# The inverse of the delta rule: both 64-row halves of a product in one PSUM bank, and one instruction to empty it

## The reference

```python
k_beta = kc * bc[..., None]
kk = jnp.einsum('nbhik,nbhjk->nbhij', k_beta, kc) * seg
a_mat = jnp.eye(L, dtype=F32) + jnp.where(strict, kk, 0.0)
rhs = jnp.concatenate([v_beta, k_beta * jnp.exp(b)[..., None]], axis=-1)
sol = lax.linalg.triangular_solve(a_mat, rhs, left_side=True, lower=True)
u, w = sol[..., :V], sol[..., V:]
...
def step(S, xs):
    v_new = u_c - jnp.einsum('bhik,bhkv->bhiv', w_c, S)
    o = jnp.einsum('bhik,bhkv->bhiv', q_d, S) + jnp.einsum('bhij,bhjv->bhiv', a_c, v_new)
    S = S * jnp.exp(bl)[..., None] + jnp.einsum('bhjk,bhjv->bhkv', k_o, v_new)
    return S, o
```

## Time and profile before

| what | us |
|---|---|
| three runs, median (lowest to highest) | 2605.27 (2598.81 to 2605.86) |
| span of the profiled execution | 2602.8 |
| PE busy in it | 2444.8 (94%) |
| DVE, ACT, POOL busy | 1348.7, 916.7, 785.7 |
| `phase_mix_c`, first key transpose to the end | 1750.05 to 2602.8 |
| one steady tile of it, from Y(0,0) to the next Y(0,0) | 2058.16 to 2105.30, so 47.14 |

### The profile page before, as it was taken

One profiled execution on the slowest core, in us unless ns is written; L12 is line 12 of the kernel. 1 busy time (PEld: TensorE's weight loads), 2 busy tenths in 40 slices (PEclk: granted clock), 3 DMA queues, 4 the chain that ended last, 5 costly groups with the idle time before them and its releaser, 6 DMA issues. The chain is left out here.

```text
span 2602.8 us, 53223 instructions
## 1 busy us (share of the span) xinstructions
PE 2444.8 (94%) x20756; PEld 1476.9 (57%) x20756; DVE 1348.7 (52%) x2949; ACT 916.7 (35%) x2636; POOL 785.7 (30%) x847
## 2 busy tenths in 40 slices
PE   6989999997999977999999999987999999999998
PEld 2434444444565533444444444456787887878876
DVE  3422222122678844992634626436566675666666
ACT  3633232322111114442322322235455554544541
POOL 2540000021111103550000000007456465565554
PEclk8999999998999997999999999998999999999998
DMA  8541212134544553551121121126222231221313
GB/s 296 156 142 45 89 49 77 42 121 138 210 153 147 172 178 111 164 153 66 65 74 49 61 88 49 57 67 192 73 91 83 67 107 59 83 91 59 95 35 94
DMA packets 254517, 270.02 MB, mean 104 GB/s; under 512 B 30263, under 2 KB 188023, under 8 KB 254314
## 3 DMA queue, kind: packets, MB, share of 16 engines
q1 hardware_dynamic: 186762, 219.27, 25.8%
q10 hardware_dynamic: 67552, 47.84, 6.7%
HBM read 179.70 MB, written 87.36 MB: 103 GB/s over the span
## 5 line engine op out<-in xcount | busy, mean ns | idle before, releaser
L625 PE MATMUL inc_b<-raw_next,inc_w_hi 128*128 128x512 bf16 (+1 forms) x768 | 229.9, 381 | 1.6 <-POOL inc_w_lo L574 1.6
L625 PE MATMUL inc_b<-keep,inc_w_hi 128*128 128x512 bf16 (+1 forms) x768 | 228.4, 379 | 0.0
L625 PE MATMUL inab_b<-inab_wt,keep 128*128 128x512 f16 x768 | 168.4, 381 | 10.6 <-POOL inab_wt L574 10.6
L625 PE MATMUL inab_b<-inab_wt,raw_next 128*128 128x512 f16 x768 | 166.4, 379 | 0.0
L1171 PE MATMUL mixab_y<-keep,mixab_oT_hi 128*128 128x512 f16 x512 | 153.4, 381 | 7.4 <-DVE mixab_f_y L1251 5.7
L2173 DVE SCALAR_TENSOR_TENSOR inc_acc<-inc_ub,inc_taps,inc_acc 128x512 f32<-128x512 f32 x192 | 152.1, 792 | 6.8
L625 PE MATMUL inc_b<-raw_next,inc_w_lo 128*128 128x512 bf16 x384 | 146.3, 381 | 0.0
L625 PE MATMUL inc_b<-keep,inc_w_lo 128*128 128x512 bf16 x384 | 145.6, 379 | 0.0
L2071 ACT ACTIVATE inc_ub<-inc_b 128x512 f32<-128x512 f32 x96 | 56.9, 593 | 251.1 <-PE inc_b L625 251.1
L2169 DVE COPY inc_ub<-inc_halo 128x3 f32<-128x3 f32 x96 | 26.1, 272 | 228.1 <-ACT inc_ub L2071 228.1
L625 PEld LDWEIGHTS inab_b<-inab_wt,keep 128*128 128x128 bf16 (+1 forms) x768 | 75.4, 98 | 101.4 <-issue 13.2
(11 more groups left out here) (590 smaller groups left out, 6085.4 us busy)
## 6 DMA issues: line engine op xcount, KB each, us to landing
tmp_qkv<-stage_next SPq DMA_DIRECT2D x98, 256.0 KB, 2.0
stage_next<-in_w_in_c ACTq DMA_DIRECT2D x30, 512.0 KB, 4.5
inab_stage<-in_w_in_ab ACTq DMA_DIRECT2D x24, 512.0 KB, 4.0
raw_next<-tmp_qkv SPq DMA_DIRECT2D x8, 1536.0 KB, 6.9
mixc_qkv<-tmp_qkv SPq DMA_DIRECT2D x8, 1536.0 KB
inab_wt<-in_w_ada SPq DMA_DIRECT2D x10, 1024.0 KB, 14.7
keep<-in_x_prompt SPq DMA_DIRECT2D x16, 512.0 KB, 4.1
tmp_v<-inab_vz SPq DMA_DIRECT2D x32, 256.0 KB, 4.1
```

The costliest lines, as they stand in the source:

```text
L625: last = nc.tensor.matmul(dst, lhs(a, k), rhs(b, k), start=(k == 0 and i == 0), stop=(k == KT - 1 and i == len(PASSES) - 1))
```

## The change

Both halves of a product go to one bank, at their own partitions: Y to A0 (g = 0) or C0 (g = 1), T and N to B0 (g = 0) or C1 (g = 1). One DVE instruction over 128 partitions writes `Y`, one ACT instruction copies `T`, and one copies `N`; DVE's copies of `T` and `N` at levels 0 to 3 go. So that an instruction over 128 partitions can write both halves of `N`, the inverse stays in the compact `N0` through the levels, and the last level's result alone is copied to `N` (low half by ACT, high half by DVE, now the full 64 columns). `first_inverse` goes, and `tn_products` of level 0 waits for `N0` itself. `y_product` no longer waits for copies of `N`. The keys of g = 1 are transposed first, into B1, which the levels leave free. All matmuls remain.

```diff
-    LY = [[half_view(x)[:, 0:4] for x in pair] for pair in ((A0, A1), (C0, C1))]
-    LT = [[half_view(x)[:, 0:4] for x in pair] for pair in ((B0, B1), (C0, C1))]
-    LN = [[half_view(x)[:, 4:8] for x in pair] for pair in ((B0, B1), (C0, C1))]
+    LY = [half_view(x)[:, 0:4] for x in (A0, C0)]
+    LT = [half_view(x)[:, 0:4] for x in (B0, C1)]
+    LN = [half_view(x)[:, 4:8] for x in (B0, C1)]
...
-        def first_inverse(t, halves):
...
         def evacuate(t, k, g, halves, widths):
...
-            if not final or w == LEVELS[-1]:
-                act.activation(blocks(T[HALF[0], gs(g), :], w, 0), blocks(LT[g][0][HALF[0]], w, 0), ACT.Copy).then_inc(t_lo, 1)
-            if not final and g == 0 and 1 in halves:
-                act.wait_ge(t_hi, nth(t, g, NL - 1, k))
-            for e in halves if g == 0 else LOW:
-                last = act.activation(blocks(N[HALF[e], gs(g), HALF[e]], w, 1), blocks(LN[g][e][HALF[e]], w, 1), ACT.Copy)
-            last.then_inc(n_ready, 1)
+            if not last_width or w == LEVELS[-1]:
+                rows = HALF[0] if last_width or halves == LOW else slice(0, P)
+                act.activation(blocks(T[rows, gs(g), :], w, 0), blocks(LT[g][rows], w, 0), ACT.Copy).then_inc(t_copied, 1)
+            if last_width:
+                act.activation(N[HALF[0], gs(g), HALF[0]], LN[g][HALF[0]], ACT.Copy).then_inc(n_low, 1)
+            else:
+                act.activation(blocks(N0[rows, gs(g), :], w, 1), blocks(LN[g][rows], w, 1), ACT.Copy).then_inc(n_copied, 1)
...
-        for g in GRP:
+        for g in KEY_GRP:
             key_squares(0, 0, P, g)
             key_copy(0, 0, P, g)
         last_decay(0, 0, 0, P)
         for g in GRP:
             decays(0, 0, P, g)
-        first_inverse(0, BOTH)
         query_squares(0, P)
...
-            for e in halves:
-                rows = HALF[e]
-                last = dve.tensor_tensor(blocks(Y[w][rows, gs(g), :], w, 0), blocks(LY[g][e][rows], w, 0),
-                                         bc(eye[rows], [HB, 4, HB // (2 * w), w]), ALU.add)
-            last.then_inc(y_ready, 1)
...
+            dve.tensor_tensor(blocks(Y[w][rows, gs(g), :], w, 0), blocks(LY[g][rows], w, 0),
+                              bc(eye, [HB if halves == LOW else P, 4, HB // (2 * w), w]), ALU.add).then_inc(y_ready, 1)
...
+            if k == len(widths) - 1 and 1 in halves:
                 dve.wait_ge(tn_mm, nth(t, g, NL, k))
-                dve.tensor_copy(blocks(T[HALF[1], gs(g), :], w, 0), blocks(LT[g][1][HALF[1]], w, 0)).then_inc(t_hi, 1)
-            if 1 in halves and g == 1:
-                dve.wait_ge(tn_mm, nth(t, g, NL, k))
-                dve.tensor_copy(blocks(N[HALF[1], gs(g), HALF[1]], w, 1), blocks(LN[g][1][HALF[1]], w, 1)).then_inc(n1_hi, 1)
+                dve.tensor_copy(N[HALF[1], gs(g), HALF[1]], LN[g][HALF[1]]).then_inc(n_high, 1)
...
-        dve.wait_ge(n0_copied, nth(nt, 1))
+        dve.wait_ge(tn_mm, nth(nt, 1, NL, 1))
...
-                if 1 in halves:
-                    pe.wait_ge(t_hi, nth(t, g, NL - 1, k - 1))
-                if g == 1:
-                    evacuated(t, k - 1, g, halves)
-                wait_apart(pe, t_lo, nth(t, g, NL, k - 1), fin.tick)
+                wait_apart(pe, t_copied, nth(t, g, NL, k - 1), fin.tick)
...
-                pe.wait_ge(n0_copied, nth(t, g))
+                pe.wait_ge(n0_ready, nth(t, g))
             else:
-                evacuated(t, k - 1, g, halves)
+                pe.wait_ge(n_copied, nth(t, g, NL - 1, k - 1))
...
-                        mm(LT[g][e][rows, i, :], N[rows, h, rows], Y[w][rows, h, :], start=True, stop=True)
-                    last = mm(LN[g][e][rows, i, :], Y[w][rows, h, :], N[rows, h, rows], start=True, stop=True)
+                        mm(LT[g][rows, i, :], N0[rows, h, :], Y[w][rows, h, :], start=True, stop=True)
+                    last = mm(LN[g][rows, i, :], Y[w][rows, h, :], N0[rows, h, :], start=True, stop=True)
...
                 if k == 2:
-                    turn_k(t + 1, nxt, half, n2, 0)
+                    turn_k(t + 1, nxt, half, n2, 1)
...
-            turn_k(t + 1, nxt, half, n2, 1)
+            turn_k(t + 1, nxt, half, n2, 0)
```

More of the change, by code:

```diff
@@ L2402, in phase_mix_c @@
         "gram", "qk_done", "ebl_ready", "lsub", "lseg_ready", "seg_ready", "segw_ready", "bt_ready", "attn_ready"))
[L2403 to L2406, removed]
+    n0_half, n0_ready, t0_ready, btm_ready, y_init = (s(n) for n in (
+        "n0_half", "n0_ready", "t0_ready", "btm_ready", "y_init"))
+    y_mm, y_ready, tn_mm, t_copied, n_copied, n_low, n_high = (s(n) for n in (
+        "y_mm", "y_ready", "tn_mm", "t_copied", "n_copied", "n_low", "n_high"))
     y64_mm, y64_ready, n64_mm, n64_ready = s("y64_mm"), s("y64_ready"), s("n64_mm"), s("n64_ready")
@@ L2895, in y_part, with n_part @@
             w = widths[k]
-            eye = blocks(tv["eye_h"].unsqueeze(1), w, 0)
+            rows = HALF[0] if halves == LOW else slice(0, P)
+            eye = blocks(tv["eye_h"][rows].unsqueeze(1), w, 0)
             dve.wait_ge(y_mm, nth(t, g, NL, k))
-            for e in halves:
-                rows = HALF[e]
-                last = dve.tensor_tensor(blocks(Y[w][rows, gs(g), :], w, 0), blocks(LY[g][e][rows], w, 0),
-                                         bc(eye[rows], [HB, 4, HB // (2 * w), w]), ALU.add)
-            last.then_inc(y_ready, 1)
-        def t_part(t, k, g, halves, widths):
-            w = widths[k]
-            if 1 in halves and k < len(widths) - 1:
+            dve.tensor_tensor(blocks(Y[w][rows, gs(g), :], w, 0), blocks(LY[g][rows], w, 0),
+                              bc(eye, [HB if halves == LOW else P, 4, HB // (2 * w), w]), ALU.add).then_inc(y_ready, 1)
+        def n_part(t, k, g, halves, widths):
+            if k == len(widths) - 1 and 1 in halves:
                 dve.wait_ge(tn_mm, nth(t, g, NL, k))
-                dve.tensor_copy(blocks(T[HALF[1], gs(g), :], w, 0), blocks(LT[g][1][HALF[1]], w, 0)).then_inc(t_hi, 1)
-            if 1 in halves and g == 1:
-                dve.wait_ge(tn_mm, nth(t, g, NL, k))
-                dve.tensor_copy(blocks(N[HALF[1], gs(g), HALF[1]], w, 1), blocks(LN[g][1][HALF[1]], w, 1)).then_inc(n1_hi, 1)
+                dve.tensor_copy(N[HALF[1], gs(g), HALF[1]], LN[g][HALF[1]]).then_inc(n_high, 1)
         def levels(t, halves, widths, beside=lambda k: None):
@@ L3097, in turn_k @@
             pe.wait_ge(tile_in[par], 32 * (half + 1) if not isinstance(t, int) or t else 16)
-            if t:
-                pe.wait_ge(t_lo, nth(t - 1, 0, NL, NL - 1))
-                pe.wait_ge(n_ready, nth(t - 1, 0, NL, NL - 1))
+            if t and g == 1:
+                pe.wait_ge(attn_ready, nth(t - 1, 1))
+            elif t:
+                pe.wait_ge(t_copied, nth(t - 1, 0, NL, NL - 1))
+                inverse_ready(t - 1, 0)
             for i, h in heads(g):
@@ L3140, in turn_o, with inverse_ready @@
                 last.then_inc(o_turned, 1)
-        def evacuated(t, k, g, halves):
-            pe.wait_ge(n_ready, nth(t, g, NL, k))
-            if g == 1 and 1 in halves:
-                pe.wait_ge(n1_hi, NL * t + k + 1)
+        def inverse_ready(t, g):
+            pe.wait_ge(n_low, nth(t, g))
+            pe.wait_ge(n_high, nth(t, g))
         def y_product(t, k, g, halves, widths):
@@ L3162, in y_product @@
                     rows = HALF[e]
-                    last = mm(LY[g][e][rows, i, :], BTm[w][rows, h, :], T[rows, h, :], start=True, stop=True)
+                    last = mm(LY[g][rows, i, :], BTm[w][rows, h, :], T[rows, h, :], start=True, stop=True)
             last.then_inc(y_mm, 1)
@@ L3177, in tn_products @@
                     rows = HALF[e]
[L3178 to L3180 removed]
+                    if not last_width or (w == LEVELS[-1] and e == 0):
+                        mm(LT[g][rows, i, :], N0[rows, h, :], Y[w][rows, h, :], start=True, stop=True)
+                    last = mm(LN[g][rows, i, :], Y[w][rows, h, :], N0[rows, h, :], start=True, stop=True)
             last.then_inc(tn_mm, 1)
@@ L3210, in across_n @@
         def across_n(t):
-            evacuated(t, NL - 1, 1, BOTH)
+            for g in GRP:
+                inverse_ready(t, g)
             wait_apart(pe, y64_ready, t + 1, fin.tick)
```

36 lines of the change are left out of this document (15 added, 21 removed).

## The result

The kernel after takes 2574.53 us (median of 4 runs, 2569.45 to 2583.57) beside 2605.57 for the kernel before on the same chip (4 runs). The ratio is 0.9888, with a 95% interval from 0.9864 to 0.9911. 2571 was predicted, with 2560 to 2588 as the range. The sum went by the span, and there the agreement looks better still: 2568.6 against 2567.6. In part that is luck: the profiled execution was the fastest of the four, and its agreement hides errors that cancel, as the stretches of the phase show. The kernel after was profiled twice; the second execution is that of the run `c4_after_again`, the same program on another chip.

What follows compares the result with a forecast made beforehand. PE bounds the kernel: fully busy for 26.70 us of a steady tile, with waits in the 20.44 us of levels. 16 tiles at 1.91 (30.6) plus 3.6 ahead of tile 0 save 34.2 us: 2571 us, range 2560 to 2588.

Steps and rivals of the forecast that it cites:

- rival 1: Levels: halves writing one bank take turns, 12 us a tile more, 192 in all, near 2797 us; chance 0.09.
- Y by one instruction: Level rounds: one DVE instruction takes 0.29 us, so TN(k,1) starts 1.27 after Y(k,1) rather than 1.57.
- The N wait: Ahead of Y(k,1) in the levels: without waiting for DVE's N copy, it starts 0.95 us behind TN(k,0), 0.18 less.
- Beyond the two waits above this is worth nothing in a steady tile: Steady tile: removed DVE and ACT work gains nothing besides the Y and N waits; it lies beside PE's work.
- The text's own floor: One level round without waiting: two TN groups of 0.95 and two Y groups of 0.58, 3.06 us against 3.65.
- The end of the levels: From Y(4,1) to TN(4,1), key transpose between: 1.27 us in place of 1.56, 0.29 saved per tile.
- Ahead of tile 0: Before Y(0,0) of tile 0: without first_inverse the query squares start earlier, 3.6 us saved (bounds 0 and 5.71).
- The sample tile has low halves only and gains nothing: Sample tile, after the 16 prompt tiles: the change is worth nothing there.
- The part on moved work: DVE and ACT copies dropped or widened, keys of g = 1 first: worth nothing in a steady tile beyond the two waits.
- Rival 2: Level rounds: only one of the two waits goes, 11.5 or 10 us less gain, 2583 or 2581 us; chance 0.13.
- rival 3: Steady tile: no change that can be told, the gaps reappear in PE's 26.70 us of projection work; chance 0.03.
- Rival 4: Stalls of issue, 3.16 us in tile 1, shift the time a few us either way; widens the range, no chance given.

Runs made afterwards that it cites:

- c2_all_but_bank: Kernel after with everything undone (two Y instructions, copies shared out, old key order, ScalarE's first copies) except the one bank and N's compact target: 2617.46 us, ratio 1.0053.
- c1_copies_split: Kernel after with the levels' T and N copies shared out over ACT and DVE as before, with PE's waits for them; one bank kept: 2595.47 us, ratio 0.9963.
- b2_n_wait: Kernel after with PE's wait for ACT's copy of N(k-1,1) put back ahead of Y(k,1): 2575.85 us, ratio 0.9884.
- a2_before_wait: Kernel before with one added wait: DVE's identity-pair copy waits for the sample tile's last TN group: 2614.66 us, ratio 1.0032 to the kernel before.
- b1_y_two: Kernel after with DVE's Y again by two instructions, one per 64-partition half, out of one bank: 2591.0 us, ratio 0.9936.
- b4_key_order: Kernel after with the next tile's keys transposed in the old order, heads 0 to 3 first: 2581.62 us, ratio 0.9911.
- b3_first_copies: Kernel after with ACT's first_inverse copies of N0 restored at their old places in every tile: 2577.05 us, ratio 0.9881.
- a3_pool_behind: Kernel after with POOL's residual add of the last tile but one held back until DVE's first four decayed-state products are done: 2570.89 us, ratio 0.9863.
- a4_eye_own: Kernel after with the identity pair in SBUF space of its own, so its copy keeps its place without the wait for PE: 2566.26 us, ratio 0.9839.

## Why the prediction was right, and where it was wrong

**Two halves in one bank (rival 1): right.** The groups keep their pace, 0.95 us for 32 records, and `c2_all_but_bank` is back at the kernel before to 0.2 us a tile. The Trainium skill, "TensorEngine Tiling (Array Packing)", Restrictions and Gotchas, says that different row tiles cannot access the same PSUM bank simultaneously. By that rule, had the chip kept it by taking turns, a TN group would take 2.04 us by the prediction's estimate; the trace has 0.95. Here, where the two row tiles write different partitions of the bank, the chip does not take turns.

**Y by one instruction: mechanism right.** 0.29 us, as taken; undoing it alone costs 0.96 to 1.10 us a tile.

**The N wait: right place, wrong reading of what carries it.** The 0.18 us are real, `c1_copies_split` shows them (1.13 in place of 0.95). But the wait alone is free (`b2_n_wait`): it was late because DVE had a copy of N behind its copy of T. What paid was that one engine empties both halves.

**"Beyond the two waits above this is worth nothing in a steady tile": wrong.** This is the step that failed for the tiles. The round was predicted as 3.65 less two separately priced waits, 3.17, and one term was carried over from the kernel before: 0.26 us from DVE's end to TN. It measured 0.10. That accounts for 0.16 of the 0.17 us between 3.17 and the 3.00 measured. Moving the copies is what changed it. It is 0.25 or 0.26 in the kernel before, `a2_before_wait`, `c1_copies_split` and `c2_all_but_bank`, which share the copies out, and 0.10 in the kernel after and all other runs, where ACT has them alone. Whether PE stands idle does not decide it: in `b1_y_two` PE is idle for 0.10 us ahead of TN and the term is 0.10, in `c1_copies_split` PE is busy to within 0.01 us and it is 0.26. With the copies also went entries of PE's own wait lists ahead of TN(k,1), the one for DVE's copy of N among them. Whether these make the 0.16 us, no run here holds apart.

The text's own floor, 2 x 0.95 + 2 x 0.58 = 3.06, would have been the nearer forecast: PE is busy for all 17.88 us. Three rounds of 0.65 make 1.95, the end 0.36 (1.56 to 1.20, 0.29 predicted), and the rest, 0.24, is the entry, for which 0.18 was predicted: 2.55 in an undisturbed tile. Over 16 tiles that would be 41 us. Stalls of issue in some tiles (2.33 and 2.31 in the means of tiles 2 to 15) left 36.4 and 35.1, not 30.6.

**The end of the levels: right.** The key order is needed for it: `b4_key_order` loses 0.43 us of it again. The prediction priced this, without saying that it hangs on the key order.

**Ahead of tile 0: right in size there, its worth open.** 3.67 us against 3.6, the copies are the cause (`b3_first_copies`), and DVE's scaled values bound Y(0,0) as forecast, with 2.12 us of wait. But by Y(0,0) of tile 2 it can't be told any more: from the start of the phase 112.3 us with the copies, and 108.0 to 113.0 in the seven profiles with tiles of the new length but without them. In tiles 0 and 1 stalls of issue of 1 to 3 us come and go. Between nothing and 3.7 us of this term is in the total.

**"The sample tile has low halves only and gains nothing": wrong, it loses 8 to 11 us in the two profiles.** The part on moved work followed the copies and the key order, but not the wait that the change moved: `eye2` lies in the space of `N0`, which the levels now use to their end, so its copy waits for PE's last product and no longer for ACT. The term that failed is the sample tile's, put at nothing. I didn't name what is queued behind that copy, and whom DVE meets there. The wait is 0.2 us; what it costs is the order of two engines. `a2_before_wait` shows that the wait suffices, `a3_pool_behind` that it is harmless when POOL isn't there, `a4_eye_own` that the loss goes with it.

The Trainium skill has this rule in "SBUF — State Buffer", Who interferes with whom: VectorE and GpSimd share a port pair, the one that starts first holds it for its whole instruction, and the other blocks; in its words, "Issue order, not op shape, decides who blocks." The traces agree that one waits for the other: 0.21 us against 2.14 for the same copy, 4.62 against 11.43 for the same four products. Which row starts first does not always tell who wins, as the last section shows. I had not weighed it, since the steady tile shows no such loss on PE's path.

Of the 8.3 us, 6.85 come by the wait for `oT_lo`: PE's first projection row behind it starts 29.82 us into the stretch, where it started 22.97 us into it before. The other 1.4 are the slow projection rows that follow. The second profile of the kernel after has the same wait (6.70) and 3.1 us more, and these are the clock. The windows of the last stretch, before, after, and after again, end with the granted clock, DMA share and GB/s:

```profile
2552.00:2602.80 50.80, 42.15 (x267) 31.04 (x264) 32.11 (x49) 8.67 (x36) 20.11 (x17) 0.81 0.40 115
```

```profile
2508.50:2567.60 59.10, 43.72 (x267) 31.24 (x266) 32.50 (x57) 8.55 (x36) 15.52 (x15) 0.78 0.33 94
```

```profile
2514.00:2576.20 62.20, 46.82 (x267) 33.47 (x266) 32.62 (x57) 8.57 (x36) 15.58 (x15) 0.74 0.32 89
```

For the same 267 records PE is busy 3.1 us longer in the last. Behind its wait of 6.7 us PE's projection rows take 0.61 to 0.63 us in place of 0.38, at a granted clock of 0.50: the lower level, 1.2 GHz. That holds for 6 matmuls in the first profile of the kernel after (the seventh takes 0.54) and for 12 in the second, before the 0.38 returns. It and the products behind it make about half of the 3.1 us. The rest lies in a second stretch at 0.50, which all three profiles have and which is some 3 us longer in the last; rows of L3308 take 0.42 us there in place of 0.27.

The first profile is on the mild side. Nine profiles of this document have the new wait with POOL free to begin; in all of them PE waits 6.7 us. The stretch is 82.0 and 82.15 us in two of them, and 84.5 to 85.8 in seven. Against the 73.9 before, the wait costs 8 to 12 us.

In sum: the median lies 3.5 us above the 2571 because a tile gain that was 4 to 6 us too small stands against a loss of 8 to 11 us that was missing. The mechanism of the main term was right; that the number came out so close was luck.

Rival 2 (only one wait goes) and rival 3 (no change) did not happen. Rival 4, stalls of issue, is the scatter of the tiles: undisturbed tiles take 44.60 us, the mean of 14 is 44.8.

## What to carry to other kernels

When a change gives a buffer a longer life, list every instruction that now waits for its new last reader, on each engine, down to the prologue and the tail; a wait of 0.2 us can cost 8 when it changes which engine comes first. Where several small waits stand in one round, compute the round without any of them as well: a cut that relieves an engine of half its instructions may reach that floor. A sum of separately priced waits carries over terms of the kernel before, such as the 0.26 us from DVE's end to the matmul behind it, and they can shrink too. Where both halves of a product lie in one bank, the gain is in the instructions and waits that go, not in the bank.
